# Index scores of a two-block transformer kernel: two heads in two 64-row halves of the array, two steps at a time, and the index keys turned inside the second chunk

## The chip, the core and the metric

The kernel runs on one core of a Trainium2 chip, as one launch. The metric is device time in microseconds (us), the median of the runs of one kernel. The engines are PE (TensorE: matmuls; PEld is its weight load), ACT (ScalarE), DVE (VectorE), POOL (GpSimd) and SP (SyncE, which here only issues DMA).

## What is computed

Two transformer blocks on 256 tokens of width 2048, all in float32. The change lies in the first block, in the scores that choose 64 keys for each query. With `q_idx` of 16 heads x 64, one shared `k_idx` of 64 and a weight for each head:

```python
proj = h @ w_in                                   # h: 256 x 2048
k_idx = _rms_norm(k_idx, k_norm_idx)              # 256 x 64, one key for all 16 heads
logits = jnp.einsum('bqhd,bsd->bqhs', qic, k_idx) * IDX_DIM ** -0.5
score = jnp.einsum('bqh,bqhs->bqs', wc, jax.nn.relu(logits)) * IDX_HEADS ** -0.5
score = jnp.where(causal[None], score, NEG_INF)
_, sel = lax.top_k(score, top_k)                  # top_k = 64, then attention over sel
```

The rest (attention of two kinds, the second block with its scan, latent attention and feed-forward) is the same in both kernels.

## The kernel before

The large products multiply a float32 activation by a float32 weight, each split in a high and a low part in a shorter float32 form. A weight matrix comes in **pieces** of 512 input rows by 512 columns. A piece is numbered `n`; SP loads it into one of four slots `WR` (L589), ACT copies its high part into `WH` (L1520, in two halves of 128x1024), POOL subtracts to get the low part `WL` (L553, two halves), and PE runs 24 matmuls of 512 columns on it (L879, L880, L881: high by high, low by high, high by low). Four pieces make one **chunk** of 512 output columns; its 16 steps of six matmuls are counted by `kk` from 0 to 15, and a hook `begin(kk)` can put other work ahead of a step (`tok_chunk`, L883). `WH` has two buffers: a half of piece n+2 can be written only when PE has finished the same half of piece n. Every engine runs its own list in order and waits on semaphores.

The first block's `w_in` is done as four column groups interleaved with the adaptive norm (they hold the index queries and keys, and as fourth group the first chunk), then as chunks `j` = 1 to 7 for the one kind of attention (b = 0) and 0 to 7 for the other (b = 1). Index queries end up in `QI` (eight pairs of heads, 256 columns each; a pair fills the 128 rows, one head on rows 0 to 63, the other on 64 to 127).

**The index keys.** ACT reads the key rows and head weights into `KI` (L1602). DVE squares, sums and scales (L1964 to L1971), ACT taking the square root between (L1528). DVE writes the normed keys into `KIX`, which holds for each half `t` of the tokens two 128x128 tiles: one with the keys in columns 0 to 63 and zeros behind, one with zeros ahead and the keys in columns 64 to 127; the zeros were set by POOL at the start (L727). PE turns the four tiles into bank 4 (L1044), ACT copies the bank into `KB` (L1618, 128 x 2 x 256), and PE waits for that (L1071, `kb_ready`) ahead of chunk 1. In ACT's list the copy stands ahead of the read of the first chunk's banks (L1533) and of the high parts of chunk 1's third piece.

**The index steps.** In chunks 5 and 6 of b = 0, ahead of every second step (`kk` odd), PE runs one index step `s` (0 to 15; pair of heads `s // 2`, token half `t = s % 2`): one matmul (L1055) of a pair's 128 rows by `KB`, both of its parts, into bank `4 + t`, 2 x 128 or 2 x 256 columns. The zeros keep the two heads apart. Step 0 waits until ACT has emptied bank 4 of an earlier use (`headT_taken` 6); step s from 2 on waits for `relu_ready` of step s-2. ACT applies the relu of the step (L1627), one before each half of a high part; DVE multiplies by the head's weight and adds (L1987, L1989). At the end of chunk j for j = 1 to 4, PE turns the normed heads into banks 4 and 5 or 6 and 7 (L1082), and ACT takes them (L1662), counted by `headT_taken`, two each time.

Of the kernel before, what the change touches and what calls it, by code (L numbers as in the profile page):

```python
# [22 lines left out]
ACT = mybir.ActivationFunctionType  # L23
# [3 lines left out]
P = 128  # L27
L = 256
TT = L // P
# [3 lines left out]
HEADS = 8  # L33
# [12 lines left out]
PIECES = KT // PK  # L46
CH = 512
# [87 lines left out]
def build(nc, a, out):  # L135
    ctx = ExitStack()
    with ctx:
# [86 lines left out]
        KIT = at(23200, L)  # L224
        KIX = at(22176, TT, 2, P)
        KB = at(22688, 2, L)
        relu = at(23200, 2, CH)
# [479 lines left out]
        def _(pool):  # L707
# [16 lines left out]
            for h in range(2 * HEADS):  # L724
                pool.memset(slope[:, h:h + 1], float(np.float32(2.0 ** (-8.0 * (h % HEADS + 1) / HEADS)))) \
                    .then_inc(consts_set, 1)
            pool.memset(KIX[:, :, :, :], 0.0).then_inc(consts_set, 1)  # L727

# [123 lines left out]
            lows(n_dn, n_end)  # L852
        CONSTS = 1 + 4 + 2 * HEADS + 1


        @block.tensor
        def _(pe):
# [181 lines left out]

            pe.wait_ge(act_took, 4)  # L1040
            pe.wait_ge(kix_ready, 4)
            for lo in range(2):
                for t in range(TT):
                    last = pe.transpose(BANK[4][:, lo * L + t * P:lo * L + (t + 1) * P], KIX[:, t, lo, :], ident[:])  # L1044
            last.then_inc(kixT_ready, 1)

            def index_step(s):

                j, t = s // 2, s % 2
                w = (t + 1) * P  # L1050
                if s == 0:
                    pe.wait_ge(headT_taken, 6)
                if s >= 2:
                    pe.wait_ge(relu_ready, s - 1)
                pe.matmul(BANK[4 + t][:, 0:2 * w].rearrange("p (a n) -> p a n", a=2), QI[:, j, t * P:(t + 1) * P], KB[:, :, 0:w],  # L1055
                          start=True, stop=True).then_inc(idx_ready, 1)

            def index_from(s):

                def begin(kk):  # L1060
                    if kk % 2 == 1:
                        index_step(s + kk // 2)
                return begin

            for b in range(2):
                for j in range(8):

                    if b == 0 and j == 0:
                        continue
                    if b == 0 and j == 1:  # L1070
                        pe.wait_ge(kb_ready, 1)  # L1071
                    pe.wait_ge(act_took, b * 16 + 6 + 2 * j - 2)
                    tok_chunk(n_br + PIECES * j, (j + 1) % 2, CH, more=b * (8 * PIECES),
                              **(dict(begin=index_from(8 * (j - 5))) if b == 0 and j in (5, 6) else {}))
                    if 1 <= j <= 4:
# [425 lines left out]
        def _(act):  # L1501
# [115 lines left out]
            act.wait_ge(kixT_ready, 1)  # L1617
            act.activation(KB.rearrange("p a n -> p (a n)"), BANK[4][:, :], ACT.Copy).then_inc(kb_ready, 1)  # L1618

            def index_relu(s):  # L1620

                t = s % 2
                w = (t + 1) * 2 * P
                act.wait_ge(idx_ready, s + 1)
                if s >= 2:
                    act.wait_ge(relu_used, s - 1)
                act.activation(relu[:, t, 0:w], BANK[4 + t][:, 0:w], ACT.Relu).then_inc(relu_ready, 1)  # L1627

# [266 lines left out]
        def _(dve):  # L1895
# [73 lines left out]
            for t in range(TT):  # L1969
                for lo in range(2):  # L1970
                    dve.scalar_tensor_tensor(out=KIX[:, t, lo, lo * IDX_DIM:(lo + 1) * IDX_DIM], in0=KI[:, t, 0:IDX_DIM],  # L1971
                                             scalar=krstd[:, t:t + 1], in1=kin_g, op0=ALU.mult,
                                             op1=ALU.mult).then_inc(kix_ready, 1)


            def choose_keys():

                for s in range(16):
                    j, t = s // 2, s % 2
                    w = (t + 1) * P  # L1980
                    sc = score[:, 0:P] if t == 0 else score[:, P:SPAN]
                    dve.wait_ge(relu_ready, s + 1)
                    for f in range(2):
# [462 lines left out]
```

## Time and profile before

| | us |
|---|---|
| median of 3 runs | 1973.9 |
| lowest, highest | 1969.86, 1974.69 |
| profiled execution, its time | 1972.74 |
| span of that execution | 1971.0 |
| PE busy | 1882.3 (95% of the span) |
| POOL busy | 1359.9 |
| DVE busy | 1088.5 |
| ACT busy | 807.6 |

The span runs from the first to the last instruction of the profiled execution; 1.7 us lie around it. PE's busy time is an upper estimate, since the ends of pipelined matmuls are modelled: the distance from the start of one matmul to the start of the next says what it costs. A float32 matmul that isn't split stands in the trace as two records; a transpose is one record. The granted clock of PE is at full speed for most of the span, with some stretches at half.

### The profile page before, as it was taken

The numbers are of one execution on the slowest core, as the hardware profiler recorded it, in microseconds if no ns is written. First come the engines' busy times: TensorE is split into PE (matmuls) and PEld (weight loads), VectorE is DVE, ScalarE is ACT, GpSimd is POOL, SyncE is SP. The second block draws the span as 40 slices with busy tenths as digits, with TensorE's granted clock in tenths as the row PEclk, the third lists the DMA queues.
The fourth block names the chain that finished last, engine by engine and source line by source line (L and its number), as shares of the span: only waits on it lengthen the run. The fifth ranks groups of instructions, "written<-read, shape, count | busy, mean of one in ns | idle before, by whom it ended". The sixth has DMA issues, their size and how long they took to land.

```text
span 1971.0 us, 32237 instructions
## 1 busy us (share of the span) xinstructions
PE 1882.3 (95%) x12919; PEld 1569.5 (80%) x12919; DVE 1088.5 (55%) x1156; ACT 807.6 (41%) x1095; POOL 1359.9 (69%) x683
## 2 busy tenths in 40 slices
PE   5889999999989999989999999999999999999997
PEld 2667878888657898878699777888888888888886
DVE  1015647551354546976644375777888888923223
ACT  3234444444444554333422445434333343333333
POOL 2547877888329889963544498899999998844442
PEclk9999999999999999999999999999999999999999
DMA  9984544555765565543100145555555555555553
GB/s 330 382 295 158 185 171 171 192 183 187 266 239 171 163 190 193 192 150 109 45 24 4 67 164 168 203 192 186 178 189 191 180 182 191 170 192 192 192 192 128
DMA packets 174432, 352.58 MB, mean 179 GB/s; under 512 B 6735, under 2 KB 19421, under 8 KB 171773
## 3 DMA queue, kind: packets, MB, share of 16 engines
q1 hardware_dynamic: 173437, 346.94, 51.9%
q10 hardware_dynamic: 896, 4.20, 0.5%
q8 instruction: 77, 1.26, 0.3%
q14 instruction: 22, 0.18, 0.0%
HBM read 349.02 MB, written 2.10 MB: 178 GB/s over the span
## 4 chain that ended last, share of the span: by engine, by line
PE 59%; POOL 17%; issue 16%; DVE 6%; ACT 1%; POOLq 0%; DVEq 0%; ACTq 0%
PE bank L925 19%; POOL WL L553 17%; PE bank L927 10%; PE bank L879 7%; PE bank L881 6%; PE bank L880 6%; PE bank L1300 6%; PE bank L1220 1%; PE bank L1230 1%; DVE CV L2362 1%; DVE CV L2367 1%; PE bank L991 1%; PE bank L1263 1%; DVE AL L2343 0%; DVE arena L2110 0%
## 5 line engine op out<-in xcount | busy, mean ns | idle before, releaser
L553 POOL TENSOR_TENSOR WL<-WR,WH 128x1024 fp32r<-128x1024 f32 (+2 forms) x516 | 1262.7, 2468 | 435.4 <-ACT WH L1520 433.8
L1520 ACT ACTIVATE WH<-WR 128x1024 fp32r<-128x1024 f32 (+2 forms) x560 | 576.3, 1037 | 774.4 <-PE bank L881 434.0
L925 PE MATMUL bank<-HX,WH 128*128 128x512 f32 x1840 | 648.8, 398 | 0.9 <-POOL WL L553 0.9
L927 PE MATMUL bank<-HX,WL 128*128 128x256 f32 x1840 | 515.2, 280 | 0.0
L925 PEld LDWEIGHTS bank<-HX,WH 128*128 128x128 f32 x1840 | 345.6, 188 | 86.5 <-POOL WL L553 2.1
L879 PE MATMUL bank<-WH,HX 128*128 128x512 f32 (+2 forms) x864 | 341.6, 395 | 13.6 <-POOL WL L553 8.6
L927 PEld LDWEIGHTS bank<-HX,WL 128*128 128x128 f32 x1840 | 347.1, 189 | 0.1
L881 PE MATMUL bank<-WH,HX 128*128 128x512 f32 (+2 forms) x864 | 332.9, 385 | 0.0
L880 PE MATMUL bank<-WL,HX 128*128 128x512 f32 (+2 forms) x864 | 332.6, 385 | 0.0
L879 PEld LDWEIGHTS bank<-WH,HX 128*128 128x128 f32 x864 | 163.7, 189 | 52.4 <-issue 14.0
L880 PEld LDWEIGHTS bank<-WL,HX 128*128 128x128 f32 x864 | 163.8, 190 | 31.2 <-issue 1.9
L881 PEld LDWEIGHTS bank<-WH,HX 128*128 128x128 f32 x864 | 163.6, 189 | 31.3
L553 DVE TENSOR_TENSOR WL<-WR,WH 128x1024 fp32r<-128x1024 f32 x44 | 53.8, 1225 | 155.8 <-ACT WH L1520 155.8
L879 PE MATMUL bank<-WH,AH 128*128 128x512 f32 x352 | 137.7, 391 | 1.8 <-DVE WL L553 1.8
L880 PE MATMUL bank<-WL,AH 128*128 128x512 f32 x352 | 137.6, 391 | 0.0
L881 PE MATMUL bank<-WH,AL 128*128 128x512 f32 x352 | 137.5, 391 | 0.0
L2362 DVE TENSOR_SCALAR CV<-RAWF,cols 128x256 f32<-128x256 f32 x44 | 102.0, 2378 | 2.0 <-DVE RAWF L2123 2.0
L2367 DVE SCALAR_TENSOR_TENSOR CV<-RAWF,cols,CV 128x256 f32<-128x256 f32 x44 | 96.0, 2239 | 1.6 <-DVE CV L2362 1.5
L2036 DVE TENSOR_SCALAR arena<-arena,small 128x128 f32<-128x128 f32 x64 | 63.7, 1064 | 49.6 <-ACT small L1528 49.6
L879 PEld LDWEIGHTS bank<-WH,AH 128*128 128x128 f32 x352 | 66.5, 189 | 16.0 <-DVE WL L553 2.2
L881 PEld LDWEIGHTS bank<-WH,AL 128*128 128x128 f32 x352 | 66.5, 189 | 14.0
L880 PEld LDWEIGHTS bank<-WL,AH 128*128 128x128 f32 x352 | 66.4, 189 | 13.7
(307 smaller groups left out, 2067.6 us busy)
## 6 DMA issues: line engine op xcount, KB each, us to landing
WR<-in_w_in SPq DMA_DIRECT2D x96, 1024.0 KB, 4.8
WR<-in_ffn_w_gate SPq DMA_DIRECT2D x44, 1024.0 KB, 5.0
WR<-in_ffn_w_up SPq DMA_DIRECT2D x44, 1024.0 KB, 5.0
WR<-in_ffn_w_down SPq DMA_DIRECT2D x44, 1024.0 KB, 5.0
arena<-in_w_ada SPq DMA_DIRECT2D x64, 512.0 KB, 10.4
WR<-in_w_out SPq DMA_DIRECT2D x32, 1024.0 KB, 5.1
WR<-in_w_ada SPq DMA_DIRECT2D x16, 1024.0 KB, 5.1
WR<-in_w_in SPq DMA_DIRECT2D x12, 768.0 KB, 4.2
```

The costliest lines, as they stand in the source:

```text
L553: eng.tensor_tensor(half(WL, n % NSLOT, *w), half(WR, n % NSLOT, *w), half(WH, nth(n) % 2, *w), ALU.subtract).then_inc(ready, 1)
L879: pe.matmul(out, stat[0], mov[0], start=start, stop=False, skip_group_check=True)
L880: pe.matmul(out, stat[0], mov[1], start=False, stop=False, skip_group_check=True)
L881: return pe.matmul(out, stat[1], mov[0], start=False, stop=stop, skip_group_check=True)
L925: pe.matmul(bank[:, :].rearrange("p (h n) -> p h n", h=2), wh[:, k, o], hx[:, :, kk, :], start=kk == 0, stop=False, skip_group_check=True)
L927: last = pe.matmul(bank[:, 0:L], wl[:, k, o], hx[:, 0, kk, :], start=False, stop=kk == KT - 1, skip_group_check=True)
L991: pe.transpose(o, x, ident[:]))
L1300: last = pe.matmul(o[h, q, :], x(h, q), y(h, q), start=(n == 0), stop=(n == len(terms) - 1))
L1520: act.activation(half(WH, nth(n) % 2, *w), half(WR, n % NSLOT, *w), ACT.Copy).then_inc(hi_ready, 1)
L2036: last = dve.tensor_scalar(v, v, hr[:, g:g + 1], None, ALU.mult)
L2362: own.mark(dve.tensor_scalar(CV[:, f, :], RAWF[:, f, 2:L + 2], w(2), cols[:, ds(4 * i + (cb + f), 1)], ALU.mult, ALU.add))
L2367: own.mark(dve.scalar_tensor_tensor(out=CV[:, f, :], in0=RAWF[:, f, 1:L + 1], scalar=w(1), in1=CV[:, f, :], op0=ALU.mult, op1=ALU.add))
```

## The change

`KIX` and `KB` lose the zeros: a `KIX` tile holds the keys twice, in columns 0 to 63 and 64 to 127, so that `KB` holds them on rows 0 to 63 and again on 64 to 127. PE turns two tiles and not four, inside chunk 1, ahead of `kk` = 4; the wait for `kb_ready` stands behind chunk 1. An index step is two matmuls of 64 rows, one for each head, into banks `4 + 2t` and `5 + 2t`, of 128 or 256 columns each; two steps stand together ahead of `kk` = 1, 5, 9, 13. Step 1 has a wait of its own (`headT_taken` 8). Each relu is two instructions of half the width, and the counts of `relu_ready` are doubled. POOL's memset goes.

```diff
@@ PE
-            pe.wait_ge(act_took, 4)
-            pe.wait_ge(kix_ready, 4)
-            for lo in range(2):
-                for t in range(TT):
-                    last = pe.transpose(BANK[4][:, lo * L + t * P:lo * L + (t + 1) * P], KIX[:, t, lo, :], ident[:])
-            last.then_inc(kixT_ready, 1)
+            def turn_key(kk):
+
+                if kk == 4:
+                    pe.wait_ge(act_took, 4)
+                    pe.wait_ge(kix_ready, 4)
+                    for t in range(TT):
+                        last = pe.transpose(BANK[4][:, t * P:(t + 1) * P], KIX[:, t, :], ident[:])
+                    last.then_inc(kixT_ready, 1)
...
-                if s == 0:
-                    pe.wait_ge(headT_taken, 6)
-                if s >= 2:
-                    pe.wait_ge(relu_ready, s - 1)
-                pe.matmul(BANK[4 + t][:, 0:2 * w].rearrange("p (a n) -> p a n", a=2), QI[:, j, t * P:(t + 1) * P], KB[:, :, 0:w],
-                          start=True, stop=True).then_inc(idx_ready, 1)
+                if s < 2:
+                    pe.wait_ge(headT_taken, 6 + 2 * s)
+                else:
+                    pe.wait_ge(relu_ready, 2 * (s - 1))
+                for f in range(2):
+                    half_ = slice(IDX_DIM * f, IDX_DIM * (f + 1))
+                    last = pe.matmul(BANK[4 + 2 * t + f][:, 0:w], QI[half_, j, t * P:(t + 1) * P], KB[half_, 0:w],
+                                     start=True, stop=True)
+                last.then_inc(idx_ready, 1)
...
-                    if kk % 2 == 1:
+                    if kk % 4 == 1:
                         index_step(s + kk // 2)
+                        index_step(s + kk // 2 + 1)
...
+                    pe.wait_ge(act_took, b * 16 + 6 + 2 * j - 2)
+                    tok_chunk(n_br + PIECES * j, (j + 1) % 2, CH, more=b * (8 * PIECES),
+                              **(dict(begin=index_from(8 * (j - 5)) if j > 1 else turn_key) if b == 0 and j in (1, 5, 6) else {}))
                     if b == 0 and j == 1:
                         pe.wait_ge(kb_ready, 1)
-                    pe.wait_ge(act_took, b * 16 + 6 + 2 * j - 2)
-                    tok_chunk(n_br + PIECES * j, (j + 1) % 2, CH, more=b * (8 * PIECES),
-                              **(dict(begin=index_from(8 * (j - 5))) if b == 0 and j in (5, 6) else {}))
@@ ACT
-            act.activation(KB.rearrange("p a n -> p (a n)"), BANK[4][:, :], ACT.Copy).then_inc(kb_ready, 1)
+            act.activation(KB, BANK[4][:, 0:L], ACT.Copy).then_inc(kb_ready, 1)
...
-                act.activation(relu[:, t, 0:w], BANK[4 + t][:, 0:w], ACT.Relu).then_inc(relu_ready, 1)
+                for f in range(2):
+                    act.activation(relu[:, t, f * w // 2:(f + 1) * w // 2], BANK[4 + 2 * t + f][:, 0:w // 2],
+                                   ACT.Relu).then_inc(relu_ready, 1)
@@ DVE
-                    dve.scalar_tensor_tensor(out=KIX[:, t, lo, lo * IDX_DIM:(lo + 1) * IDX_DIM], in0=KI[:, t, 0:IDX_DIM],
+                    dve.scalar_tensor_tensor(out=KIX[:, t, lo * IDX_DIM:(lo + 1) * IDX_DIM], in0=KI[:, t, 0:IDX_DIM],
...
-                    dve.wait_ge(relu_ready, s + 1)
+                    dve.wait_ge(relu_ready, 2 * (s + 1))
```

The lines of the changed kernel are one lower in `product` (L878 to L880). On PE, where chunk 1 of b = 0 begins, the list of the kernel before reads (L879 to L881 are the weight products, L1044 the turn of the keys):

```order
L880 MATMUL bank<-WL,HX 128x512
L881 MATMUL bank<-WH,HX 128x512
L1044 MATMUL bank<-ident,arena 128x128 [waits kix_ready,act_took]
L1044 MATMUL bank<-ident,arena 128x128 x3
L879 MATMUL bank<-WH,HX 128x512 [waits lo_ready,act_took,kb_ready]
L880 MATMUL bank<-WL,HX 128x512
```

In the changed kernel it reads, 24 weight matmuls (`kk` 0 to 3) further on:

```order
L879 MATMUL bank<-WL,HX 128x512
L880 MATMUL bank<-WH,HX 128x512
L1045 MATMUL bank<-ident,arena 128x128 [waits kix_ready,act_took]
L1045 MATMUL bank<-ident,arena 128x128
L878 MATMUL bank<-WH,HX 128x512 [waits lo_ready]
L879 MATMUL bank<-WL,HX 128x512
```

The turn moved behind the first piece of chunk 1, and the first matmul of the chunk waits for the keys no more. On PE, in chunk 5, ahead of `kk` = 1, before:

```order
L880 MATMUL bank<-WL,HX 128x512
L881 MATMUL bank<-WH,HX 128x512
L1055 MATMUL bank<-arena 128x256 [waits headT_taken]
L879 MATMUL bank<-WH,HX 128x512
L880 MATMUL bank<-WL,HX 128x512
```

And in the changed kernel, at the same place (L1058 is an index matmul, of 64 rows in and 128 rows out):

```order
L879 MATMUL bank<-WL,HX 128x512
L880 MATMUL bank<-WH,HX 128x512
L1058 MATMUL bank<-arena 128x128 [waits headT_taken]
L1058 MATMUL bank<-arena 128x128
L1058 MATMUL bank<-arena 128x256 [waits headT_taken]
L1058 MATMUL bank<-arena 128x256
L878 MATMUL bank<-WH,HX 128x512
```

The second step came forward from `kk` = 3, with a wait for the last two reads of L1662. On ACT, around the start of chunk 5, the changed kernel reads (L1538 reads a chunk's banks, L1669 takes the turned heads, L1633 is the relu, L1525 the high part):

```order
L1538 ACTIVATE arena<-bank 128x512 [waits piece_done]
L1538 ACTIVATE arena<-bank 128x512
L1669 ACTIVATE arena<-bank,small 128x512 [waits headT_ready]
L1669 ACTIVATE arena<-bank,small 128x512
L1633 ACTIVATE arena<-bank 128x128 [waits idx_ready]
L1633 ACTIVATE arena<-bank 128x128
L1525 ACTIVATE WH<-WR 128x1024 [waits half_done,piece_in2]
L1633 ACTIVATE arena<-bank 128x256 [waits idx_ready]
L1633 ACTIVATE arena<-bank 128x256
```

Against the kernel before, ACT's list has only each relu cut in two; nothing else in it moved.

## Rows read from the trace of the kernel before

**Rows 1.** Page, part 1: busy us (share of the span) and instructions.

```profile
PE 1882.3 (95%) x12919; PEld 1569.5 (80%) x12919; DVE 1088.5 (55%) x1156; ACT 807.6 (41%) x1095; POOL 1359.9 (69%) x683
```

**Rows 2.** Timeline of PE, start of chunk 1: start us, us, line, tiles, idle before.

```profile
164.51 0.39 PE L881 MATMUL bank<-WH,HX 128*128 128x512 f32 x1
168.91 1.09 PE L1044 MATMUL bank<-ident,arena 128*128 128x128 f32 x4 [4.01 <-DVE arena L1971]
170.68 0.79 PE L879 MATMUL bank<-WH,HX 128*128 128x512 f32 x1 [0.69 <-ACT arena L1618]
...
174.64 0.40 PE L879 MATMUL bank<-WH,HX 128*128 128x512 f32 x1
...
179.87 0.39 PE L881 MATMUL bank<-WH,HX 128*128 128x512 f32 x1
```

**Rows 3.** Stretches: length, busy of PE, PEld, DVE, ACT, POOL, PE's clock, DMA.

```profile
167.80:174.50 6.70, 4.91 (x13) 3.76 (x14) 3.72 (x5) 1.58 (x3) 0.87 (x1) 0.50 0.22 84
```

**Rows 4.** Timeline of ACT around the turn of the keys.

```profile
161.88 1.07 ACT L1608 ACTIVATE arena<-bank 128x512 f32<-128x512 f32 x2
...
170.03 0.60 ACT L1618 ACTIVATE arena<-bank 128x512 f32<-128x512 f32 x1 [4.04 <-PE bank L1044]
170.52 1.08 ACT L1533 ACTIVATE arena<-bank 128x512 f32<-128x512 f32 x2
```

**Rows 5.** Timeline of DVE, same stretch and the scaling of chunk 1.

```profile
162.01 6.75 DVE L1971 SCALAR_TENSOR_TENSOR arena<-arena,small 128x64 f32<-128x64 f32 x4 [0.27 <-ACT small L1528]
171.64 1.23 DVE L2029 TENSOR_TENSOR arena<-arena 128x1024 f32<-128x1024 f32 x1 [2.88 <-ACT arena L1533]
...
184.89 8.15 DVE L2036 TENSOR_SCALAR arena<-arena,small 128x128 f32<-128x128 f32 x8 [10.33 <-ACT small L1528]
```

**Rows 6.** Timeline of POOL: low parts, nine in a row.

```profile
147.30 21.38 POOL L553 TENSOR_TENSOR WL<-WR,WH 128x1024 fp32r<-128x1024 f32 x9
```

**Rows 7.** Timeline of PE: two transposes in a stream of 256-column matmuls.

```profile
153.30 0.38 PE L1037 MATMUL bank<-ident,arena 128*128 128x128 f32 x2
...
153.63 0.28 PE L880 MATMUL bank<-HX,WH 128*128 128x256 f32 x1
```

**Rows 8.** Timeline of PE in chunk 5: index steps 0 and 1.

```profile
264.64 0.59 PE L1055 MATMUL bank<-arena 128*128 128x256 f32 x2
...
265.30 0.40 PE L880 MATMUL bank<-WL,HX 128*128 128x512 f32 x1
...
267.82 1.02 PE L1055 MATMUL bank<-arena 128*128 128x512 f32 x2
...
268.90 0.39 PE L880 MATMUL bank<-WL,HX 128*128 128x512 f32 x1
```

**Rows 9.** Timeline of ACT at the start of chunk 5.

```profile
264.50 1.27 ACT L1662 ACTIVATE arena<-bank,small 128x512 f32<-128x512 f32 x2
...
266.72 1.06 ACT L1520 ACTIVATE WH<-WR 128x1024 fp32r<-128x1024 f32 x1 [0.68 <-PE bank L881]
```

**Rows 10.** Timeline of PE: 16 float32 matmuls of 256 columns, 64-row halves.

```profile
878.48 3.72 PE L1189 MATMUL bank<-arena,WR 64*128 64x256 f32 x32 [2.62 <-issue]
```

**Rows 11.** The same view: 16 float32 matmuls of 256 columns on all 128 rows.

```profile
892.01 7.17 PE L1220 MATMUL bank<-arena,WR 128*128 128x256 f32 x32 [0.93 <-ACT arena L1554]
```

**Rows 12.** Weight loads, 128-row and 32-row products of 256 columns in turn.

```profile
971.23 0.29 PEld L1263 LDWEIGHTS bank<-arena,WR 32*128 32x128 f32 x2 [0.33 <-issue]
971.85 0.30 PEld L1263 LDWEIGHTS bank<-arena,WR 128*128 128x128 f32 x2 [0.33 <-issue]
```

**Rows 13.** Timeline of PE: four 32-column products at once between full ones.

```profile
133.59 0.28 PE L881 MATMUL bank<-HX,WL 128*128 128x256 f32 x1
133.80 1.07 PE L948 MATMUL bank<-arena 128*32 128x512 f32 x8
...
135.13 0.39 PE L880 MATMUL bank<-WL,HX 128*128 128x512 f32 x1
```

**Rows 14.** The same view: an idle of PE ahead of such a group.

```profile
118.72 1.06 PE L948 MATMUL bank<-arena 128*32 128x512 f32 x8 [1.71 <-DMA arena<-in_w_ada]
...
119.94 0.28 PE L880 MATMUL bank<-HX,WH 128*128 128x256 f32 x1
```

**Rows 15.** What PE waited for from 174 us on: us, times, longest.

```profile
PE bank L879 <- POOL WL L553: 8.6, 8, 2.8
```

More of the change, by code:

```diff
@@ L224, in build @@
         KIT = at(23200, L)
-        KIX = at(22176, TT, 2, P)
-        KB = at(22688, 2, L)
+        KIX = at(22176, TT, P)
+        KB = at(22688, L)
         relu = at(23200, 2, CH)
@@ L726, in _ @@
                     .then_inc(consts_set, 1)
-            pool.memset(KIX[:, :, :, :], 0.0).then_inc(consts_set, 1)
             def low(n, more=0):
@@ L852, in _ @@
             lows(n_dn, n_end)
-        CONSTS = 1 + 4 + 2 * HEADS + 1
+        CONSTS = 1 + 4 + 2 * HEADS
         @block.tensor
```

## The prediction

> **What bounds the kernel now.** I read the parts of the page first: PE is busy for 95% of the span [rows 1], so the end moves by what PE's list gets shorter or by what PE waits less. The chain of waits is of little use here, since POOL's low parts and PE's matmuls run at nearly one pace and the chain goes through either. So I went to PE's timeline at the two places that the diff touches, then to the engines that PE waits for there.
>
> First place, the turn of the keys [rows 2]. The last matmul ahead of it starts at 164.51. PE then idles for 4.01 us until DVE has written the keys, turns them, and waits again until ACT has copied them; chunk 1 starts at 170.68. From there to 174.64 there are 9 steps from one matmul to the next in 3.96 us, 0.44 us each; from 174.64 to 179.87 there are 23 in 5.23 us, 0.227 us each. The clock row says why: it is 0.50, the lower level (1.2 GHz), from 167.8 to 174.5 [rows 3], and it fell some 3 us into PE's idle time.
>
> Second place, the index steps. A step of `kk` is six matmuls, 6 x 0.227 = 1.36 us. Step 0 begins at 264.64 and the second matmul behind it at 265.30; without it that one would stand at 264.64 + 0.227 = 264.87. It costs 0.43 us. Step 1 the same way: 268.90 - (267.82 + 0.23) = 0.85 us [rows 8]. Eight pairs: 8 x 1.28 = 10.2 us, all on PE, which doesn't wait there.
>
> **The turn, part by part.** With the wait gone, chunk 1 can start 0.23 us after 164.51, at 164.74, if nothing else is late. The next in line are: the banks of the queries, which ACT has read at 161.88 + 1.07 = 162.95 [rows 4]; and the low parts. Nine of them run back to back to 147.30 + 21.38 = 168.68, 2.38 us each [rows 6]; the last four are the halves of chunk 1's first two pieces, ready at about 161.5, 163.9, 166.3 and 168.7. PE wants them at `kk` 0, 2, 4, 6: 164.7, 167.5, 170.2 and 172.9 or later. All in time. The tenth matmul then starts at 164.74 + 9 x 0.227 = 166.78 in place of 174.64: 7.86 us. The idle being gone, I take the full clock for it.
>
> The turn itself now stands in the stream at 164.74 + 4 x 1.36 = 170.2. DVE's keys are done at 162.01 + 6.75 = 168.76 [rows 5], so PE doesn't wait. Two transposes in a stream: started at 153.30, the second 256-column matmul behind them at 153.63 [rows 7], against 153.42 without: 0.21 us. Net gain 7.86 - 0.21 = **7.65 us**.
>
> What is queued behind the new place of ACT's copy: the reads of chunk 0's banks and the high parts of piece 3 of chunk 1. The transposes end at about 170.6. The copy is half as wide (some 0.3 us from the 0.49 between the starts of L1618 and L1533), the two reads take 0.48 us to issue each [rows 4], so the high part starts at 171.9; it takes 1.06 us [rows 9], and the low part 2.40 behind it: 175.4. PE wants it at `kk` 8, 164.74 + 8 x 1.36 + 0.21 = 175.8. Hidden, with 0.4 us to spare; the following halves are each 2.40 us of POOL against 2.72 of PE. If the cover fails it costs some tenths once. DVE's square of that chunk can start at 172; it took 1.23 us with POOL idle and may take twice that now; the 8.15 us of scaling [rows 5] would end at about 185.5, chunk 1 at 186.7. Hidden too, by 1 us.
>
> **The index steps, part by part.** The two heads of a step go to different 64-row halves and different banks. Does the array run them at once? The trace has this shape in float32: 16 matmuls of 64 rows and 256 columns take 3.72 us [rows 10], where 16 of 128 rows take 7.17 [rows 11]. So two halves cost what one costs. A pair of steps is then half of 1.28, 0.64 us, if the change of shape is free.
>
> It isn't. Where 128-row and 32-row products take turns, each two loads start 0.62 us apart (971.23 to 971.85) [rows 12], though 256 columns cost 7.17 / 16 = 0.45 at most, 0.43 by the index step: 0.2 us for a change, 0.4 for there and back. Where four 32-column products stand between full ones, the second full matmul starts at 135.13 [rows 13]; without the group it would stand at 133.59 + 0.12 + 0.23 = 133.94, so the group costs 1.19 us for 0.85 of columns, 0.34 for both changes. I take 0.37, between the two. With 8 pairs: 8 x (0.64 + 0.37) = 8.1 us.
>
> The page TensorEngine Tiling (Array Packing) of the Trainium skill, section Key Properties, says that changing the tiling mode, not just the tile, drains the engine; it gives no time. It speaks against putting 64-row matmuls among 128-row ones. With no price for it the sum would be 8 x 0.37 = 3.0 us better; the trace agrees that there is one.
>
> Added wait: step 1 stands at `kk` 1 and wants `headT_taken` 8, the second read of L1662. Those reads run from 264.50 to 265.77 [rows 9], while PE is there at 264.64. Step 0 needs 0.1 + 0.21 us, until 264.95; then PE waits until about 265.8, **0.85 us**, once. What is queued behind: the rest of the chunk, and ACT's first relu is no earlier anyway. Later pairs wait for both relus of the pair before. The odd one is done some 3.3 us after the pair (one `kk` of 1.36, a high part of 1.06, two relus of 0.4), and PE is back after 4 x 1.36 = 5.4 us: free. ACT's relus get some 0.3 us per pair longer and stand ahead of high parts; PE's list, 5.45 + 1.0 us per piece against 4.8 on POOL, leaves room for that. So the steps cost 8.1 + 0.85 = 8.9 us in place of 10.2: **1.3 us** gained. Bounds: halves at once with free changes and no wait, 8 x 0.64 = 5.1, a gain of 5.1; halves one after another, 8 x (1.28 + 0.37) + 0.85 = 14.0, a loss of 3.8.
>
> POOL's memset, the narrower copy and the last relu cost or give nothing: POOL is idle at the start, and the choice of keys is wanted only after eight further chunks.
>
> **Sum.** 7.65 + 1.3 = 9.0 us. What lies behind is issued relative to PE's progress (loads by `piece_done`, high parts by `half_done`), and PE waits for low parts only 8.6 us in all [rows 15], none of it against a fixed time; I carry the gain to the end whole. Against the profiled execution: 1972.74 - 9.0 = 1963.7. That execution was 1.2 us below the median of the three runs, so against the median 1973.9 - 9.0 = 1964.9. A measurement of this kernel can tell about 0.3%, 5.9 us, from no change, that is below 1968.0 or above 1979.8.
>
> **Rivals.**
>
> A: the halves don't run at once, or not with four matmuls in a row. For it: the shape seen was a long run of 16, here there are groups of four. Against: the halves of [rows 10] start together from the first, and the short group of [rows 13] does as well. Gain 7.65 - 3.8 = 3.9 us: 1970.0. Within 0.3%.
>
> B: the turn becomes a wait in its new place. The high part of `kk` 8 has 0.4 us to spare; POOL and PE then run at 2.66 and 2.72 us for a half, so a delay would be kept, not healed. If ACT were 3 us late there (the reads behind a wait that I don't see), 9.0 - 2.6 = 6.4 us remain: 1967.5. For it: the spare is thin. Against: every term of it is a row.
>
> C: slower, by the clock. In the changed kernel PE stops or half fills the array nine times in 55 us. If each of the eight groups were followed by a stretch at 1.2 GHz of 3.4 us (half the length of the one in [rows 3]), each would cost 1.7 us: 13.6 - 9.0 = 4.6 us lost, 1978.5. It decides from six stretches on. Against: after an idle time of 1.71 us and a group of narrow products, the matmuls go on at the full pace (118.72 + 1.06, then 119.94) [rows 14]; here the longest stop is 0.85 us.
>
> D: the gain is eaten or the low-clock stretches elsewhere fall differently: 3 to 5 us either way, 1969.5 for the lower gain.
>
> **Chances.** Forecast (1961 to 1967.9) 0.72; A 0.09; B 0.05, still faster by over 0.3% in most of it; D 0.10; C 0.04. Faster by over 0.3%: the forecast and most of B, 0.76; within 0.3%: A, D and the part of C with fewer than eight stretches, 0.21; slower by over 0.3%: 0.03 of C, in which the stretches are longer than I priced. The range reaches down to the best bound of the index steps (5.1 in place of 1.3: 1961.1, and some tenths for the clock elsewhere: 1960.5) and up to A (1970.0, rounded up to 1970.5); C lies outside.
>
> **What would show it.** Right: in the changed trace PE has no idle between the last matmul of chunk 0 and `kk` 0 of chunk 1, no stretch at the low clock there, chunk 1 ends some 7.6 us earlier; the two transposes stand alone without a wait; the first group of index matmuls has an idle of 0.8 us in its middle and seven later groups cost about 1.0 us each. Wrong: a low part or a high part named as releaser at `kk` 8 of chunk 1 (B), 1.6 us for a group (A), a clock of 0.50 within chunks 5 and 6 (C), or both gains there and gone by the end of the first block (D).

## The result, and the profile after

The changed kernel is not faster but slightly slower: the median of 20 runs is 1975.47 us (1971.95 to 1987.31), that of 20 runs of the kernel before beside them 1972.45 us (1968.83 to 1977.38). The ratio is 1.0021, with a 95% interval of 1.0011 to 1.0031, so +2.2 to +6.1 us. The forecast was 1964.9 us, and 1975.47 lies above the range that went with it, 1960.5 to 1970.5. The profiled execution of the changed kernel took 1973.95 us, with a span of 1972.1.

The page's first part shows what was to be expected of the work. DVE is busy for 11 us more than in [rows 1], with the same number of instructions, but that sum alone says little: the same kernel before, profiled again (e10), has 1076.4 us, 12 less than in [rows 1].

```profile
PE 1881.6 (95%) x12949; PEld 1570.1 (80%) x12949; DVE 1099.5 (56%) x1156; ACT 807.5 (41%) x1111; POOL 1359.8 (69%) x682
```

PE's timeline from the last matmul of chunk 0 into chunk 2 (start, us, line, tiles, idle ahead and what ended it); it answers to [rows 2]:

```profile
166.00 0.39 PE L880 MATMUL bank<-WH,HX 128*128 128x512 f32 x1
166.23 0.39 PE L878 MATMUL bank<-WH,HX 128*128 128x512 f32 x1
...
171.44 0.40 PE L880 MATMUL bank<-WH,HX 128*128 128x512 f32 x1
171.68 0.38 PE L1045 MATMUL bank<-ident,arena 128*128 128x128 f32 x2
...
172.13 0.39 PE L879 MATMUL bank<-WL,HX 128*128 128x512 f32 x1
...
188.03 0.39 PE L880 MATMUL bank<-WH,HX 128*128 128x512 f32 x1
...
193.78 1.94 PE L1087 MATMUL bank<-ident,arena 128*128 128x128 f32 x8 [5.37 <-DVE arena L2043]
...
195.38 0.78 PE L878 MATMUL bank<-WH,HX 128*128 128x512 f32 x1
...
199.79 0.43 PE L879 MATMUL bank<-WL,HX 128*128 128x512 f32 x1
```

The turn does what the prediction said: chunk 1 starts 0.23 us behind chunk 0, the two transposes stand in the stream without a wait, and the chunk runs at the full clock (granted clock 1.00 from 166 to 188 us). But behind chunk 1 a wait of 5.37 us has come up. There PE transposes the heads of chunk 1, and they come from DVE's scaling (L2043). The ten steps behind it take 4.41 us, 0.44 us each, where ten steps at the full clock take 2.3. The stretch behind that wait, in the columns of [rows 3]:

```profile
193.50:200.00 6.50, 6.21 (x19) 5.28 (x20) 2.87 (x5) 1.27 (x2) 0.00 (x0) 0.51 0.00 0
```

The granted clock is 0.51, the lower level, as it was in [rows 3] behind the old wait. The same place in the kernel before:

```profile
194.15 0.39 PE L881 MATMUL bank<-WH,HX 128*128 128x512 f32 x1
194.38 1.04 PE L1082 MATMUL bank<-ident,arena 128*128 128x128 f32 x8
195.17 0.48 PE L879 MATMUL bank<-WH,HX 128*128 128x512 f32 x1
```

So the sum over the two chunks, from rows, is:

| stretch | before, us | after, us | gain |
|---|---|---|---|
| last matmul of chunk 0 to last of chunk 1 | 194.15 - 164.51 = 29.64 | 188.03 - 166.00 = 22.03 | 7.61 |
| from there to the first of chunk 2 | 195.17 - 194.15 = 1.02 | 195.38 - 188.03 = 7.35 | -6.33 |
| next ten steps of chunk 2 | 197.55 - 195.17 = 2.38 | 199.79 - 195.38 = 4.41 | -2.03 |

The 7.61 us are given back and 0.75 more. Behind this, the index groups save 1.4 us (below), and the profiled execution was already 1.5 us later at 166.00, ahead of every edit on PE's path: 0.75 - 1.4 + 1.5 = 0.85 us. At the end of chunk 6, where ACT begins to read its banks, the changed kernel is 0.93 us behind (319.96 against 319.03). The two profiled executions differ by 1.2 us; the last 0.3 come up later and are not explained.

Why is the scaling late? The timelines of ACT, DVE and POOL of the changed kernel in this stretch, in this order:

```profile
172.10 0.39 ACT L1623 ACTIVATE arena<-bank 128x256 f32<-128x256 f32 x1 [4.61 <-PE bank L1045]
172.38 1.08 ACT L1538 ACTIVATE arena<-bank 128x512 f32<-128x512 f32 x2
173.34 2.97 ACT L1525 ACTIVATE WH<-WR 128x1024 fp32r<-128x1024 f32 x3
```

```profile
173.50 1.23 DVE L2036 TENSOR_TENSOR arena<-arena 128x1024 f32<-128x1024 f32 x1 [3.16 <-ACT arena L1538]
...
178.76 14.88 DVE L2043 TENSOR_SCALAR arena<-arena,small 128x128 f32<-128x128 f32 x8 [1.50 <-ACT small L1533]
```

```profile
174.49 18.87 POOL L553 TENSOR_TENSOR WL<-WR,WH 128x1024 fp32r<-128x1024 f32 x8 [4.23 <-ACT WH L1525]
```

ACT waits 4.61 us for the turn, and behind its copy stand the high parts of chunk 1's third piece. The first starts 7.3 us behind the last matmul of chunk 0 and the second 8.3; in e9 (below), where ACT makes them first, they start 3.2 and 5.9 us behind it (169.40 and 172.07, against 166.19). POOL, which wants them, is idle for 4.23 us until 174.49 and then has eight low parts to make up: 18.87 us with no gap. All but the last of the eight scalings lie inside that, and they take 14.88 us, where they took 8.15 in [rows 5]. The durations of the eight (shortest, middle, longest in ns), after and then before:

```profile
L2043 DVE TENSOR_SCALAR arena<-arena,small x8: 275/2402/2432, 178.8 to 193.4; 128x128 f32<-128x128 f32 x8
```

```profile
L2036 DVE TENSOR_SCALAR arena<-arena,small x8: 275/276/2474, 184.9 to 192.8; 128x128 f32<-128x128 f32 x8
```

One scaling takes 0.275 us, or 2.4 us, which is the length of one low part of POOL. Before, five of the eight were short; after, six were long, and each of these six ends 0.08 us behind the end of a low part of POOL. In the kernel before POOL stood with small gaps in this stretch, since ACT's high parts came just in time:

```profile
184.84 2.40 POOL L553 TENSOR_TENSOR WL<-WR,WH 128x1024 fp32r<-128x1024 f32 x1 [0.26 <-ACT WH L1520]
187.62 2.40 POOL L553 TENSOR_TENSOR WL<-WR,WH 128x1024 fp32r<-128x1024 f32 x1 [0.39 <-ACT WH L1520]
```

The theory (called theory T in the expectations) is then: while POOL has a queue, each DVE instruction of this kind waits for the end of a low part, and only one gets in at each end; a gap in POOL lets some more in. What the change did is to let ACT's high parts run late. POOL is then behind, and works with no gap, a low part each 2.36 us, to catch up with PE, which wants one each 2.72 us.

The section "Who interferes with whom" of the Trainium skill's page SBUF — State Buffer says that VectorE and GpSimd share one pair of ports, that some tensor_scalar forms take it, and that whoever comes first holds it for the whole instruction while the other stands. The trace agrees: 2.40 us is a whole POOL instruction, and in e4 (below) it is POOL that stands, for 1.0 us. The prediction had not drawn on it.

### The profile page after: what moved, and what is told of

Its sections match the earlier page's. It is cut to its first block, busy times and chain, and to the rows that moved or that the text cites. A ratio compares the mean times of both kernels' runs of the same rounds, so it can differ in the third digit from the quotient of the medians.

```text
span 1972.1 us, 32313 instructions
## 1 busy us (share of the span) xinstructions
PE 1881.6 (95%) x12949; PEld 1570.1 (80%) x12949; DVE 1099.5 (56%) x1156; ACT 807.5 (41%) x1111; POOL 1359.8 (69%) x682
## 3 DMA queue, kind: packets, MB, share of 16 engines
q8 instruction: 78, 1.28, 0.3%
## 4 chain that ended last, share of the span: by engine, by line
PE 59%; POOL 17%; issue 16%; DVE 6%; ACT 1%; POOLq 0%; DVEq 0%; ACTq 0%
PE bank L924 19%; POOL WL L553 16%; PE bank L926 10%; PE bank L878 7%; PE bank L880 7%; PE bank L879 7%; PE bank L1305 6%; PE bank L1225 1%; PE bank L1235 1%; DVE CV L2369 1%; DVE CV L2374 1%; PE bank L990 1%; PE bank L1268 1%; DVE AL L2350 0%; DVE arena L2117 0%
## 5 line engine op out<-in xcount | busy, mean ns | idle before, releaser
L1525 ACT ACTIVATE WH<-WR 128x1024 fp32r<-128x1024 f32 (+2 forms) x560 | 576.1, 1037 | 779.0 <-PE bank L880 437.0
L878 PE MATMUL bank<-WH,HX 128*128 128x512 f32 (+2 forms) x864 | 337.5, 391 | 12.7 <-POOL WL L553 8.6
L880 PE MATMUL bank<-WH,HX 128*128 128x512 f32 (+2 forms) x864 | 332.9, 385 | 0.0
L879 PE MATMUL bank<-WL,HX 128*128 128x512 f32 (+2 forms) x864 | 332.8, 385 | 0.0
L878 PEld LDWEIGHTS bank<-WH,HX 128*128 128x128 f32 x864 | 163.7, 189 | 52.3 <-issue 14.7
L880 PEld LDWEIGHTS bank<-WH,HX 128*128 128x128 f32 x864 | 163.6, 189 | 31.2
L879 PEld LDWEIGHTS bank<-WL,HX 128*128 128x128 f32 x864 | 163.8, 190 | 29.2
L878 PE MATMUL bank<-WH,AH 128*128 128x512 f32 x352 | 137.7, 391 | 2.0 <-DVE WL L553 2.0
L880 PE MATMUL bank<-WH,AL 128*128 128x512 f32 x352 | 137.7, 391 | 0.0
L879 PE MATMUL bank<-WL,AH 128*128 128x512 f32 x352 | 137.5, 391 | 0.0
L2043 DVE TENSOR_SCALAR arena<-arena,small 128x128 f32<-128x128 f32 x64 | 70.5, 1169 | 48.7 <-ACT small L1533 48.7
L878 PEld LDWEIGHTS bank<-WH,AH 128*128 128x128 f32 x352 | 66.5, 189 | 16.4 <-DVE WL L553 2.5
L879 PEld LDWEIGHTS bank<-WL,AH 128*128 128x128 f32 x352 | 66.5, 189 | 13.9
L880 PEld LDWEIGHTS bank<-WH,AL 128*128 128x128 f32 x352 | 66.4, 189 | 13.7
```

The lines of the kernel that those rows point to most:

```text
L878: pe.matmul(out, stat[0], mov[0], start=start, stop=False, skip_group_check=True)
L879: pe.matmul(out, stat[0], mov[1], start=False, stop=False, skip_group_check=True)
L880: return pe.matmul(out, stat[1], mov[0], start=False, stop=stop, skip_group_check=True)
L1525: act.activation(half(WH, nth(n) % 2, *w), half(WR, n % NSLOT, *w), ACT.Copy).then_inc(hi_ready, 1)
L2043: last = dve.tensor_scalar(v, v, hr[:, g:g + 1], None, ALU.mult)
```

## The experiments

**Which part of the change costs?** The turn alone, put into the kernel before, with the index steps as they were:

```diff
-            pe.wait_ge(act_took, 4)
-            pe.wait_ge(kix_ready, 4)
-            for lo in range(2):
...
+            def turn_key(kk):
+
+                if kk == 4:
+                    pe.wait_ge(act_took, 4)
+                    pe.wait_ge(kix_ready, 4)
+                    for lo in range(2):
...
-                    if b == 0 and j == 1:
-                        pe.wait_ge(kb_ready, 1)
                     pe.wait_ge(act_took, b * 16 + 6 + 2 * j - 2)
                     tok_chunk(n_br + PIECES * j, (j + 1) % 2, CH, more=b * (8 * PIECES),
...
+                    if b == 0 and j == 1:
+                        pe.wait_ge(kb_ready, 1)
```

> The kernel before with the turn of the keys alone moved into chunk 1 (four tiles with zeros, index steps as before). Theory T (POOL, started late, runs back to back through chunk 1, so that each of DVE's eight scalings takes as long as one low part): the scaling takes about 15 us in place of 8.15, PE idles about 5 us ahead of L1082's turn and then runs at the low clock; time 1 to 3 us above the kernel before. Rival R (the index groups of 64 rows cost what the moved turn gives): no idle behind chunk 1, time 7 to 8 us below. Rival S (the scaling only starts late): idle of 1 to 2 us, scaling of about 8 us, time 3 to 5 us below.

Measured: 1976.19 us (1971.27 to 1983.78), ratio 1.0020 [1.0007, 1.0033]; the profiled execution was the longest of the twelve. (Every ratio here is to the kernel before, run beside it, with its 95% interval in brackets.) PE's wait, DVE's scaling and POOL's low parts in its trace:

```profile
PE bank L1085 <- DVE arena L2039: 5.6, 1, 5.6
```

```profile
185.31 14.91 DVE L2039 TENSOR_SCALAR arena<-arena,small 128x128 f32<-128x128 f32 x7 [1.29 <-ACT small L1531]
```

```profile
181.25 18.89 POOL L553 TENSOR_TENSOR WL<-WR,WH 128x1024 fp32r<-128x1024 f32 x8 [4.95 <-ACT WH L1523]
```

(The view ends at 200 us and holds seven of the eight scalings; all eight take 15.1 us.) The slowdown is all in the turn, and all of its parts are there: an idle POOL, eight low parts in a row, 15.1 us of scaling, 5.6 us of wait.

The other half, the index steps and the zero-free keys, with the turn ahead of chunk 1 as before:

```diff
+            turn_key(4)
+
...
                     if b == 0 and j == 1:
                         pe.wait_ge(kb_ready, 1)
+                    pe.wait_ge(act_took, b * 16 + 6 + 2 * j - 2)
...
-                              **(dict(begin=index_from(8 * (j - 5)) if j > 1 else turn_key) if b == 0 and j in (1, 5, 6) else {}))
+                              **(dict(begin=index_from(8 * (j - 5))) if b == 0 and j in (5, 6) else {}))
```

> The changed kernel with the turn of the keys back ahead of chunk 1 (two tiles, index steps in 64-row halves in pairs). Theory T: 1 to 1.5 us below the kernel before (two transposes fewer, index groups 0.9 us less in all); chunk 1's scaling takes 8 us. Rival R: 7 to 9 us above the kernel before. Rival S says nothing of it.

Measured: 1969.55 us, 0.9983 [0.9972, 0.9993], a gain of 1.4 to 5.5 us. So this half does help, and rival R (the index groups cost what the turn gives), which wanted 7 to 9 us lost here, falls. The turn in its trace:

```profile
169.51 0.41 PE L1045 MATMUL bank<-ident,arena 128*128 128x128 f32 x2 [1.12 <-DVE arena L1980]
...
170.39 0.50 PE L878 MATMUL bank<-WH,HX 128*128 128x512 f32 x1 [0.47 <-ACT arena L1625]
```

The idle ahead of the turn is 1.12 us here, not the 4.01 of [rows 2]. The kernel before itself, run again as e10, will show the same.

**Is it ACT's order?** The high parts of piece 3 and the read of chunk 0 moved ahead of ACT's wait for the turn, all else as in the changed kernel:

```diff
             high(n_br + PIECES + 1)
+            read_chunk(n_br, 1, [stage[:, 0, t, :] for t in range(TT)])
+            high(n_br + PIECES + 2)
             act.wait_ge(kixT_ready, 1)
...
                     if b or j:
-                        high(n + 2, more, **relus(0))
+                        if b or j > 1:
+                            high(n + 2, more, **relus(0))
...
-                    if j < 4:
+                    if b == 0 and j == 0:
+                        pass
+                    elif j < 4:
```

> The changed kernel with ACT's list in another order: the read of chunk 0's banks and both high parts of chunk 1's third piece stand ahead of the copy of the keys. Theory T: POOL starts its next low part at about 170 and not 174.5, gets its gaps of 0.3 us back, the scaling takes 8 to 9 us, PE doesn't idle at the turn behind chunk 1 and the clock doesn't fall there; time 7 to 9 us below the kernel before, some 9 to 11 below the changed one. Rival R: same as the changed kernel within 1 us. Rival S: also a gain, but the scaling takes 8 us in the changed kernel already, which its trace denies; so a scaling of 12 us or more here, with an early start, would speak against T.

Measured: 1966.05 us (1962.66 to 1969.7), 0.9965 [0.9951, 0.9979]. This is 4.1 to 9.7 us faster than the kernel before, by the medians 5.9 where I expected 7 to 9, and the lowest median of all. POOL, DVE and PE in its trace:

```profile
179.22 2.40 POOL L553 TENSOR_TENSOR WL<-WR,WH 128x1024 fp32r<-128x1024 f32 x1 [0.26 <-ACT WH L1525]
...
182.00 2.40 POOL L553 TENSOR_TENSOR WL<-WR,WH 128x1024 fp32r<-128x1024 f32 x1 [0.39 <-ACT WH L1525]
```

```profile
179.28 8.14 DVE L2048 TENSOR_SCALAR arena<-arena,small 128x128 f32<-128x128 f32 x8 [5.18 <-ACT small L1533]
```

```profile
188.54 0.39 PE L880 MATMUL bank<-WH,HX 128*128 128x512 f32 x1
188.77 1.03 PE L1087 MATMUL bank<-ident,arena 128*128 128x128 f32 x8
```

The gaps are back, the scaling takes 8.14 us, and PE goes from chunk 1 into the transposes without a wait.

**Which of the two moves did it?** A rival (S in the expectations) blames the late read of chunk 0: DVE starts later, and a long scaling merely becomes visible. Only the read moved ahead, then only the high parts:

```diff
             high(n_br + PIECES + 1)
+            read_chunk(n_br, 1, [stage[:, 0, t, :] for t in range(TT)])
             act.wait_ge(kixT_ready, 1)
```

> The changed kernel with only the read of chunk 0's banks moved ahead of the copy of the keys on ACT; the third piece's high parts stay behind it. Theory T: POOL still starts at about 174 and runs without gaps, the scaling takes 13 to 15 us, PE idles 4 to 6 us; time as the changed kernel within 2 us. Rival S (the scaling starts late because ACT reads chunk 0 late): the wait goes, time as e3.

```diff
             high(n_br + PIECES + 1)
+            high(n_br + PIECES + 2)
             act.wait_ge(kixT_ready, 1)
```

> The changed kernel with only the two high parts of chunk 1's third piece moved ahead of the copy of the keys on ACT; the read of chunk 0's banks stays behind the copy. It is the other half of e3. Theory T: POOL starts its next low part at once, gets its gaps back, the scaling takes 8 to 9 us and PE has no idle behind chunk 1; time within 1.5 us of e3. If e3's gain needed the early read too: the scaling ends late and PE idles 1 us or more.

Measured: with the read alone one run of 1978.05 us, with the high parts alone 1967.71 us, 0.9975 [0.9964, 0.9986]. The scaling of the first, PE's wait in it, and the scaling of the second:

```profile
180.45 14.02 DVE L2046 TENSOR_SCALAR arena<-arena,small 128x128 f32<-128x128 f32 x8 [6.02 <-ACT small L1533]
```

```profile
PE bank L1087 <- DVE arena L2046: 4.5, 1, 4.5
```

```profile
179.49 7.60 DVE L2045 TENSOR_SCALAR arena<-arena,small 128x128 f32<-128x128 f32 x8 [0.28 <-ACT small L1533]
```

In the first DVE's square starts 2.5 us behind the last matmul of chunk 0, not 7.5 as in the changed kernel. The scaling doesn't start earlier for it, since ACT makes its square root behind the late high parts; it meets a POOL without gaps and takes 14.02 us. So the early read is not enough, and the time shows no gain: 1978.05 is 2.6 us above the changed kernel's median, a little more than the 2 us that I allowed, in one run. The second decides against S: the read is late there, the scaling starts no earlier either (13.3 us behind the last matmul of chunk 0, 12.8 in the changed kernel), it takes 7.60 us, and PE doesn't wait. The order of the high parts is the cause; S falls.

**Is it a wait for each instruction, or slower data?** The eight scalings made one instruction on the same data, in all chunks:

```diff
-                    for g in range(8):
-                        v = s[:, g // 4, (g % 4) * DH:(g % 4 + 1) * DH]
-                        last = dve.tensor_scalar(v, v, hr[:, g:g + 1], None, ALU.mult)
+                    v = flat.rearrange("p (g n) -> p g n", n=DH)
+                    last = dve.tensor_tensor(v, v, hr.unsqueeze(2).to_broadcast([P, 8, DH]), ALU.mult)
```

> The changed kernel with the eight scalings of a chunk done by one DVE instruction (128x1024 times a broadcast factor; for every chunk of both kinds). Theory T (an instruction of this kind waits for POOL's running one, once per instruction): 2.5 to 4 us in place of 14.9 with POOL still back to back; no idle of PE behind chunk 1; time 7 to 9 us below the kernel before. If the slow scaling came from the amount of data that DVE moves beside POOL, it would still take 8 us or more. Rival R: no change.

Measured: 1967.65 us, 0.9977 [0.9963, 0.9991], a gain of 1.8 to 7.3 us where I expected 7 to 9. DVE and POOL:

```profile
180.58 1.67 DVE L2042 TENSOR_TENSOR arena<-arena,small 128x1024 f32<-128x1024 f32 x1 [1.51 <-ACT small L1533]
```

```profile
176.30 25.70 POOL L553 TENSOR_TENSOR WL<-WR,WH 128x1024 fp32r<-128x1024 f32 x10 [4.52 <-ACT WH L1525]
```

POOL has ten low parts in a row up to 200 us, where the view ends, more than in the changed kernel, and the scaling takes 1.67 us in place of 14.88; PE doesn't wait. The next low part, whose start falls into the scaling, takes 3.40 us in place of 2.40: once DVE is in, it is POOL that waits. The amount of data is the same, so it is not that; but the operation changed with the number of instructions, and the sixteen scalings below, which keep the operation, are what shows that the number counts. The same edit in the kernel before:

> The kernel before with one DVE instruction in place of the eight scalings of a chunk, as in e4, and nothing else. Theory T: the scaling is hidden behind the chunk in the kernel before, so the time stays within 1 us of it; what e4 gained then comes from the wait that the changed kernel had. If one instruction is a gain by itself: 2 us or more below. The idle ahead of the turn of the keys (4.0 us in the trace of before, 1.1 us in that of e2) gives a third sample of how long that wait is.

Measured: 1973.39 us, 1.0002 [0.9990, 1.0014]. No difference: there the scaling is hidden, as the prediction had read it. The one instruction takes 3.43 us there, since it comes just behind the start of a low part and waits for all of it.

The opposite, sixteen scalings of 64 columns:

```diff
-                        v = s[:, g // 4, (g % 4) * DH:(g % 4 + 1) * DH]
-                        last = dve.tensor_scalar(v, v, hr[:, g:g + 1], None, ALU.mult)
+                        for e in range(2):
+                            v = s[:, g // 4, (g % 4) * DH + 64 * e:(g % 4) * DH + 64 * (e + 1)]
+                            last = dve.tensor_scalar(v, v, hr[:, g:g + 1], None, ALU.mult)
```

> The changed kernel with sixteen scalings of half the width (128x64) in place of eight. Theory T, one instruction for each of POOL's while POOL has no gap: 16 x 2.36 = 38 us for chunk 1 in place of 15, PE idle for 27 us or more behind it, time 25 us or more above the changed kernel. If the slowness follows the amount of data: 15 us again, time as the changed kernel.

Measured: one run of 2021.26 us. Chunk 1's scaling, POOL beside it, the durations of the sixteen, and PE's waits over the whole kernel:

```profile
182.00 16.14 DVE L2044 TENSOR_SCALAR arena<-arena,small 128x64 f32<-128x64 f32 x16 [1.50 <-ACT small L1533]
```

```profile
177.72 18.89 POOL L553 TENSOR_TENSOR WL<-WR,WH 128x1024 fp32r<-128x1024 f32 x8 [4.53 <-ACT WH L1525]
```

```profile
L2044 DVE TENSOR_SCALAR arena<-arena,small x16: 240/242/2445, 182.0 to 197.9; 128x64 f32<-128x64 f32 x16
```

```profile
PE bank L1087 <- DVE arena L2044: 33.1, 8, 6.6
```

I expected 38 us of scaling and 27 of idle PE in chunk 1; it is 16.14 and 6.6. The way in which that was wrong shows the rule better. The scalings wait one low part each only while POOL runs, to 177.72 + 18.89 = 196.61. Then POOL has no free buffer, since PE stands waiting and frees none; the rest take 0.24 us each. The delay limits itself in one chunk, but it is there in eight chunks: 33.1 us of wait, and 46 us over the changed kernel's median, the low clock behind the waits included (mean granted clock 0.975, 0.985 in the changed kernel).

**Do the two cures add up?** ACT's order and the single scaling together:

> The changed kernel with ACT's order of e3 and the one scaling of e4 together. Theory T: both remove the same wait, so they don't add: within 1 us of e3. If they add: 4 us below e3.

Measured: 1969.05 us (1963.92 to 1973.64), 0.9980 [0.9968, 0.9991]. No more than either alone; both take away the same wait. The median stands 3 us above that of e3, more than the 1 us that I expected. The two intervals overlap (0.9968 to 0.9979), and I read nothing from it.

**How steady is one trace?** The kernel before and the changed one once more, each as it was:

> The kernel before once more, for its trace. The idle ahead of the turn of the keys was 4.0 us in one trace and 1.1 in e5's; if 4.0 is the rarer value, the gain of moving the turn was priced too high from one trace: 2 to 3 us of it and not 7.65.

> The changed kernel once more, for its trace. Theory T: the scaling of chunk 1 takes 14 to 15 us again and PE idles 4.5 to 6 us ahead of its turn, whatever the stage before looks like.

Measured: 1972.61 and 1974.39 us. PE at the turn in the kernel before, seen again, and then PE's wait in the changed one:

```profile
169.01 0.39 PE L881 MATMUL bank<-WH,HX 128*128 128x512 f32 x1
...
170.52 0.63 PE L1044 MATMUL bank<-ident,arena 128*128 128x128 f32 x4 [1.12 <-DVE arena L1971]
...
171.83 0.50 PE L879 MATMUL bank<-WH,HX 128*128 128x512 f32 x1 [0.69 <-ACT arena L1618]
```

```profile
PE bank L1087 <- DVE arena L2043: 5.4, 1, 5.4
```

The loss in the changed kernel is steady: 5.4, 5.4 and, in e1, 5.6 us. The gain is not. Of four traces with the turn in its old place (before, e2, e5, e10), only the one that I had predicted from shows the long wait; the other three have 1.1 us, and the clock doesn't fall behind it (granted clock 1.00). There the turn costs 171.83 - 169.01 - 0.23 = 2.6 us, so taking it out of the way is worth 2.6 - 0.2 = 2.4 us, not 7.65. The 4.01 us came at least in part of the same mechanism: in that execution DVE's keys ran beside nine low parts in a row [rows 5, 6] and took 6.75 us; in e10 the same line took 5.18:

```profile
165.19 5.18 DVE L1971 SCALAR_TENSOR_TENSOR arena<-arena,small 128x64 f32<-128x64 f32 x4 [0.27 <-ACT small L1528]
```

That is 1.6 us of the 2.9 by which the two idles differ. The rest lies in DVE's small steps ahead of it: from the first square to the end of the keys it takes 13.9 us in the trace of before and 11.0 in e10. The long form is not unique to that trace. In the profiled execution of the changed kernel the keys took 6.85 us and were done 3.95 us after PE's last matmul of chunk 0, which only didn't matter because the turn had moved, and e6's trace is the same: three of thirteen. So the gain of 7.61 us is real for that pair of executions, and 2.4 us is that of the more frequent kind.

## Why the prediction was wrong

**Chunk 1 earlier: right.** 7.61 us in the trace against a forecast of 7.65; no idle, no low clock, both transposes without a wait, exactly as "what would show it" said.

**The step that failed** is the last sentence on the turn: "the 8.15 us of scaling [rows 5] would end at about 185.5, chunk 1 at 186.7. Hidden too, by 1 us." The end of chunk 1 was about right (1.3 us later than said, of which 1.5 were there from the start), but the 8.15 us is no property of the eight instructions. It is the length that POOL's gaps of 0.3 us gave them, eight times 0.275 being 2.2. The trace before would have said so: the durations in that group run from 0.275 to 2.474 us. The prediction took only their sum. I even allowed for this in the square ("may take twice that now"), which was the one operation that ran with POOL idle, and not in the scaling. Start and length both moved: start 178.76, length 14.88, end 193.64, against 188.03 for PE: 5.4 us of wait and 2.0 of low clock.

**What stood behind the new wait: right in its list, wrong in its weight.** The prediction found the high part that waits behind ACT's copy and asked if PE would get its low part in time. It did (no wait at `kk` 8). It did not ask what an idle POOL does afterwards: it has a backlog, and so no gaps, for eight low parts. Rival B named a late high part with 2.6 us lost, but it had PE waiting for POOL, not for DVE. Its premise was wrong too: the 2.66 us that it gave POOL for a half have the gap in them. Without the gap POOL takes 2.36, so the delay was healed, and DVE paid for the healing.

**The 4.01 us of idle: one execution taken for the kernel.** The gain of the turn in the more frequent kind of execution is 2.4 us. With it the sum is -2.4 + 6.33 + 2.03 - 1.4 = +4.6 us, against the +2.2 to +6.1 measured. With 7.65 it would be -0.7, outside that interval. Both errors were needed for so wrong a forecast.

**The index steps: right.** PE's timeline at two places of the kernel before, then of the changed kernel at the first group and at the first of the seven later ones (a group is two steps, so four matmuls on halves):

```profile
264.41 0.39 PE L881 MATMUL bank<-WH,HX 128*128 128x512 f32 x1
...
271.21 0.39 PE L881 MATMUL bank<-WH,HX 128*128 128x512 f32 x1
```

```profile
266.72 0.40 PE L880 MATMUL bank<-WH,HX 128*128 128x512 f32 x1
267.05 0.49 PE L1058 MATMUL bank<-arena 64*128 64x128 f32 x4
...
268.13 0.70 PE L1058 MATMUL bank<-arena 64*128 64x256 f32 x4 [0.59 <-ACT arena L1669]
...
269.10 0.39 PE L879 MATMUL bank<-WL,HX 128*128 128x512 f32 x1
...
274.12 0.39 PE L880 MATMUL bank<-WH,HX 128*128 128x512 f32 x1
274.44 0.93 PE L1058 MATMUL bank<-arena 64*128 64x128 f32 x8
...
275.63 0.39 PE L879 MATMUL bank<-WL,HX 128*128 128x512 f32 x1
...
280.65 0.39 PE L880 MATMUL bank<-WH,HX 128*128 128x512 f32 x1
```

Each stretch from the last matmul ahead of one pair or group to that ahead of the next has 24 weight matmuls, which at the full clock take 5.44 us (24 steps of (171.44 - 166.23) / 23). Before it takes 271.21 - 264.41 = 6.80, after 280.65 - 274.12 = 6.53, and the first one, with 0.59 us of idle, 274.12 - 266.72 = 7.40. So a pair cost 1.36 us and a group costs 1.09 (the forecast had 1.28, read from the first two matmuls behind each step, and 0.64 + 0.37 = 1.01), and the first group 1.96 (forecast 1.86). The gain is 8 x 1.36 - 7 x 1.09 - 1.96 = 1.3 us by these rows. ACT's reads of the banks of chunks 4 and 6 stand 55.49 us apart before (263.54 and 319.03) and 54.11 after (265.85 and 319.96), a gain of 1.4, and e10 and e2 differ by the same. The forecast was 1.3. The halves do run at once, so rival A falls, and the clock stays full (1.00 from 267 to 325 us), so rival C falls as it was put. The low clock that did come, at 0.51, followed a wait of 5.4 us.

The rule of the Trainium skill (TensorEngine Tiling (Array Packing), Key Properties) that a change of tiling mode drains the engine has a price here, if all that a group costs beyond its columns is put down to it: 1.09 - 0.64 = 0.45 us, about 0.2 us each way.

**What stays open.** From rows, e2 should gain 1.4 us by the index steps and 0.4 by two transposes fewer ahead of chunk 1 (2.16 us in its trace, 2.59 in e10): 1.8, against 1.4 to 5.5 measured. The kernels without the wait should gain 2.4 + 1.4 = 3.8. That lies inside what e4 (1.8 to 7.3), e6 (1.8 to 6.3) and e9 (2.8 to 7.1) measured, and just under e3 (4.1 to 9.7). By their medians the four gained 3.7 to 5.9 us; what is above 3.8 is not explained. A pair of traces shows how hard it is to find: e3 is 2.5 us ahead of e10 at the end of chunk 0 (166.5 and 169.0 us), before any edit on PE's path, 6.4 at about 350 us, as 2.5 + 2.4 + 1.4 says, and 7.9 at the end. What the absence of POOL's memset gives was not tried by itself, and the traces can't tell: the end of chunk 0 stands at 164.5 to 172.3 us in the four with it and at 166.0 to 169.2 in the nine without it.

## What to carry to other kernels

The duration of a group of short VectorE instructions of this kind, beside a GpSimd that is always busy, is not a property of the group but a count: take its shortest value from the group, and then count the instructions against the other engine's ends and gaps. When a wait is moved on an engine that feeds another, ask not only if the next item arrives in time but what the fed engine does with the backlog, and who lives from its gaps. An idle time that a gain rests on should be seen in more than one trace, and if it can't be, its smallest plausible size belongs in the sum.

## What was unexpected of the hardware

- A tensor_scalar of 128 columns takes 0.275 us on DVE with POOL idle and about 2.4 us with POOL busy by a subtraction of 1024 columns; so does the 64-column one (0.24 and 2.44). Only one gets in at each end of a POOL instruction if POOL has no gap. In place of eight, one tensor_tensor on the same data took 1.67 us in e4 and 3.43 in e5.
- A gap in POOL of 0.26 to 0.39 us is enough to bring eight of them from 14.88 to 8.15 us. POOL's own instructions took 2.3 to 2.5 us beside the short ones, so it is the short instructions that pay. Beside the one long instruction POOL paid as well: its next low part took 3.40 us in e4 and 2.96 in e5.
- Groups of only four float32 matmuls on two 64-row halves run at once, as in the long run of [rows 10]: a group costs 1.09 us, where the same work as products of 128 rows cost 1.36. About 0.4 us of the 1.09 are beyond its columns.
